# The last product with tokens on the partitions: x and the output gate turned in the gate stage, latent heads first

## What is computed

```python
    n_blocks = S // Q_BLOCK
    mixed = lax.map(attend_block, jnp.arange(n_blocks, dtype=jnp.int32))
    mixed = jnp.transpose(mixed, (1, 0, 2, 3)).reshape(B, S, D_MIX)
    out = (mixed * jax.nn.silu(g)) @ w_out
    return x + gate[:, None, :] * out
```

## Time and profile before

| what | value |
|---|---|
| median of 3 runs | 1884.33 us (1883.67 to 1885.18) |
| the profiled execution, its own time | 1882.65 us |
| its span, first to last instruction | 1880.8 us |
| PE busy | 1803.3 us, 96% of the span |
| DVE busy | 1026.7 us, 55% |
| ACT busy | 624.1 us, 33% |
| mean granted clock of TensorE | 0.976 of full |

### The profile page before, as it was taken

How to read it: one execution, slowest core, us unless ns; L and a number is a source line. 1 busy time by engine, 2 the same in 40 slices (tenths; PEclk the granted TensorE clock), 3 DMA queues, 4 the chain that set the end, 5 groups by cost and what they waited for, 6 DMA issues and landing times.

```text
span 1880.8 us, 22661 instructions
## 1 busy us (share of the span) xinstructions
PE 1803.3 (96%) x9123; PEld 1379.9 (73%) x9123; DVE 1026.7 (55%) x1635; ACT 624.1 (33%) x1038; POOL 70.4 (4%) x84
## 2 busy tenths in 40 slices
PE   7999999999988989999999999999999899898888
PEld 6888888878765567868888888888887554555667
DVE  5665454366366655347344457434445756647663
ACT  4221221321247651342222332222224655225420
POOL 0000000000013220000000000000000000012100
PEclk9999999999889999999999999999999999799989
DMA  6545332262000002213433333233323222101221
GB/s 222 180 157 183 112 91 83 84 204 75 23 1 1 2 22 92 79 56 90 112 90 90 98 109 90 76 115 104 98 78 107 75 78 84 46 23 49 64 90 45
DMA packets 234907, 163.59 MB, mean 87 GB/s; under 512 B 10316, under 2 KB 225588, under 8 KB 234676
## 3 DMA queue, kind: packets, MB, share of 16 engines
q1 hardware_dynamic: 232484, 157.95, 27.5%
q10 hardware_dynamic: 2320, 4.20, 0.6%
HBM read 155.84 MB, written 6.29 MB: 86 GB/s over the span
## 4 chain that ended last, share of the span: by engine, by line
PE 89%; DVE 7%; issue 1%; POOL 1%; ACT 1%; SPq 0%; DMA 0%; ACTq 0%; DVEq 0%
PE bank L896 24%; PE bank L898 23%; PE bank L897 23%; PE bank L1147 3%; PE bank L1135 2%; DVE bank L1857 2%; PE bank L1171 2%; PE bank L1311 2%; PE bank L975 1%; PE bank L1228 1%; PE bank L968 1%; PE bank L1432 1%; PE bank L1443 1%; PE bank L1102 1%; POOL Pm L503 1%
## 5 line engine op out<-in xcount | busy, mean ns | idle before, releaser
L896 PE MATMUL bank<-h_hi,w_hi 128*128 128x512 f32 x1200 | 480.1, 400 | 3.3 <-DVE h_lo L1567 2.1
L898 PE MATMUL bank<-h_hi,w_lo 128*128 128x512 f32 x1200 | 469.0, 391 | 0.0
L897 PE MATMUL bank<-h_lo,w_hi 128*128 128x512 f32 x1200 | 468.8, 391 | 0.0
L559 ACT ACTIVATE w_hi<-w_raw 128x2048 fp32r<-128x2048 f32 (+3 forms) x134 | 236.8, 1767 | 549.3 <-PE bank L898 549.3
L1512 DVE TENSOR_TENSOR w_lo<-w_raw,w_hi 128x2048 fp32r<-128x2048 f32 (+3 forms) x134 | 282.4, 2108 | 62.1 <-ACT w_hi L559 59.3
L896 PEld LDWEIGHTS bank<-h_hi,w_hi 128*128 128x128 f32 x1200 | 226.3, 189 | 75.6 <-issue 25.9
L897 PEld LDWEIGHTS bank<-h_lo,w_hi 128*128 128x128 f32 x1200 | 226.4, 189 | 49.7 <-issue 4.1
L898 PEld LDWEIGHTS bank<-h_hi,w_lo 128*128 128x128 f32 x1200 | 226.0, 188 | 47.7
L896 PE MATMUL bank<-u_hi,w_hi 128*128 128x512 f32 x352 | 138.3, 393 | 0.0
L898 PE MATMUL bank<-u_hi,w_lo 128*128 128x512 f32 x352 | 138.0, 392 | 0.0
L897 PE MATMUL bank<-u_lo,w_hi 128*128 128x512 f32 x352 | 138.0, 392 | 0.0
(11 more groups left out here) (382 smaller groups left out, 2492.3 us busy)
## 6 DMA issues: line engine op xcount, KB each, us to landing
w_raw<-in_w_in SPq DMA_DIRECT2D x28, 1024.0 KB, 5.1
w_raw<-in_ffn_w_gate SPq DMA_DIRECT2D x44, 512.0 KB, 3.7
w_raw<-in_ffn_w_up SPq DMA_DIRECT2D x44, 512.0 KB, 4.8
w_raw<-in_ffn_w_down SPq DMA_DIRECT2D x32, 704.0 KB, 4.5
ada_w<-in_ada_w SPq DMA_DIRECT2D x16, 768.0 KB, 6.2
w_raw<-in_w_in SPq DMA_DIRECT2D x21, 512.0 KB, 3.9
w_raw<-in_w_out SPq DMA_DIRECT2D x8, 1024.0 KB, 5.0
w_raw<-in_w_branch_nsa SPq DMA_DIRECT2D x8, 512.0 KB, 5.0
```

Source lines behind the costliest of these rows:

```text
L559: act.activation(w_hi[s % 2][:, 0:n], w_raw[s % 2][:, 0:n], ACT.Copy).then_inc(s_hi, 1)
L896: pe.matmul(o, l[0], r[0], start=first, stop=False)
L897: pe.matmul(o, l[0], r[1], start=False, stop=False)
L898: return pe.matmul(o, l[1], r[0], start=False, stop=last)
```

## The change

The output product now has z as the stationary operand and w_out as the moving one, so that tokens come out on the partitions and no turning is left behind it. Its slabs are four feature tiles by 512 output columns. Each half of the columns keeps four banks open over two slabs: first with z tiles 4 to 7, then with 0 to 3. Behind it DVE multiplies by a row of gates, adds x and leaves the rest to eight stores of 256 KB.

What this needs is made in the gate stage. After gate tiles 0 to 3 PE turns x, in two groups of four transposes each (`token_rows`, banks 6 and 7), and after gate tile 4 it makes the row of gates on all partitions by eight matmuls of ones with diagonal matrices, which DVE makes from the identity; ACT copies each group out of its bank. The gate tiles are made in the order 4, 5, 6, 7, 0, 1, 2, 3, the latent heads first. The spreading of the four norm rows (`widen`) is divided: two after tile 2, one each after tiles 4 and 5 of that order.

```diff
-        stage("zg", [cols_slab(wz, (c, c + 256)) for c in range(Z_G, Z_G + D, 256)], 8)
-        stage("wout2", [cols_slab(rows(A["w_out_2"][0]), (c, c + 256)) for c in range(0, D, 256)], 8)
-        stage("outT", [], 8)
+        stage("zg", [cols_slab(wz, (Z_G + c, Z_G + c + 256)) for c in (512, 768, 0, 256)], 8)
+        wo2 = rows(A["w_out_2"][0])
+        stage("wout2", [cols_slab(wo2[:, k:k + 4, :], (c, c + 512), kt=4) for c in (0, 512) for k in (4, 0)], 8)
+        stage("end", [], 0)
...
+            for i in range(2 * NT):
+                cols, t = slice(i // NT * 512, i // NT * 512 + 512), i % NT
+                sp.wait_ge(sem("osb_ready"), i + 1)
+                sp.dma_start(out[0, t * P:(t + 1) * P, cols], osb[:, t, cols]).then_inc(sem("out_stored"), 16)
...
+                for b in range(2 * i, min(2 * i + 2, N_ROWS)):
+                    dst = osb[:, b // 2, b % 2 * 512:b % 2 * 512 + 512] if b < 2 * NT else gate_row[:, 512 * (b - 2 * NT):512 * (b - 2 * NT) + 512]
+                    act.wait_ge(sem("row_full"), b + 1)
+                    act.activation(dst, row_bank(b)[:, :], ACT.Copy).then_inc(sem("row_out"), 1)
...
-                    if (s, j) == (1, 0):
-                        pe.wait_ge(sem("sstd"), 5)
-                        for h in range(4):
-                            widen(4, h, 0)
-            pe.wait_ge(sem("z_ready"), 8)
...
+            def token_rows(b):
+                if b >= 2:
+                    pe.wait_ge(sem("row_out"), b - 1)
+                for m in range(4):
+                    o = row_bank(b)[:, m * P:(m + 1) * P]
+                    if b < 2 * NT:
+                        ins = pe.transpose(o, x[:, 4 * (b % 2) + m, b // 2 * P:(b // 2 + 1) * P], ident)
+                    else:
+                        pe.wait_ge(sem("diag_ready"), 4 * (b - 2 * NT) + m + 1)
+                        ins = pe.matmul(o, ones, gate_diag[:, 4 * (b - 2 * NT) + m, :], start=m == 0, stop=m == 3)
+                ins.then_inc(sem("row_full"), 1)
+
+            for i in range(KD):
+                if i % 2 == 0:
+                    wh, wl = use_slab()
+                feature_tile(wh, wl, 0, KD, slice(i % 2 * P, i % 2 * P + P), (h_hi, h_lo))
+                if i == 0:
+                    pe.wait_ge(sem("o_free"), 16)
+                    for h in range(4):
+                        norm_sum(sum_row(0), h, True, True)
+                if i == 2:
+                    pe.wait_ge(sem("sstd"), 5)
+                    widen(4, 0, 0)
+                    widen(4, 1, 0)
+                if i in (4, 5):
+                    widen(4, i - 2, 0)
+                for b in range(2 * i, min(2 * i + 2, N_ROWS)):
+                    token_rows(b)
+            for half in range(2):
+                a0 = acc_at[0]
+                for part in range(2):
+                    wh, wl = use_slab()
+                    for t in range(NT):
+                        if part == 0:
+                            pe.wait_ge(acc_free, a0 + t - 3)
+                        if (half, part, t) == (0, 0, 0):
+                            pe.wait_ge(sem("z_ready"), 4)
+                        tokens = slice(t * P, (t + 1) * P)
+                        for k in range(4):
+                            m = Z_ORDER[4 * part + k]
+                            if (half, part, t) == (0, 1, 0):
+                                pe.wait_ge(sem("z_ready"), 5 + k)
+                            ins = mm3(bank[(a0 + t) % 4][:, :], (z_hi[:, m, tokens], z_lo[:, m, tokens]), (wh[:, k, :], wl[:, k, :]),
+                                      part == 0 and k == 0, part == 1 and k == 3)
+                        if part:
+                            close_acc(ins)
...
+            for i, m in enumerate(Z_ORDER):
+                if 3 <= i < 7:
+                    scaled(diff_out[i - 3], diff_out[i - 3], G_SUB)
+                if i + 1 < KD:
+                    scale_tile(gate_out[(i + 1) % 2][:, :])
...
+                if i < 4:
+                    for k in (2 * i, 2 * i + 1):
+                        tick(dve.tensor_scalar(gate_diag[:, k, :], ident, col[:, G_MOD + 16 + k:G_MOD + 17 + k], None, ALU.mult), "diag_ready")
+                if i % 2:
                     weights_low()
             freed()
-            for t in range(NT):
-                for half in range(2):
-                    copy_tile(osb[:, t, half * 512:(half + 1) * 512])
+            for i in range(2 * NT):
+                cols, t = slice(i // NT * 512, i // NT * 512 + 512), i % NT
+                o = (tmp, tmp2)[i % 2][:, :]
+                if i == 0:
+                    dve.wait_ge(sem("row_out"), N_ROWS)
+                free(dve.tensor_mul(o, take()[:, :], gate_row[:, cols]))
+                freed()
+                done(dve.tensor_add(osb[:, t, cols], osb[:, t, cols], o), "osb_ready")
+                if i in (1, 3):
+                    weights_low()
```

More of the change, by code:

```diff
@@ L276, in build @@
         z_lo = at("z_lo", [P, KD, S], F32R, ARENA + 32 * KB)
-        osb = at("osb", [P, NT, D], F32, ARENA + 60 * KB)
+        osb = at("osb", [P, NT, D], F32, ARENA)
+        gate_row = at("gate_row", [P, D], F32, ARENA + 48 * KB)
+        gate_diag = at("gate_diag", [P, KD, P], F32, ARENA + 52 * KB)
         bias_dram = nc.dram_tensor("bias_scratch", [4, S, S], F32, kind="Internal").ap()
@@ L373, in build @@
         block = ctx.enter_context(nc.Block())
+        Z_ORDER = [4, 5, 6, 7, 0, 1, 2, 3]
+        N_ROWS = 2 + 2 * NT
+        row_bank = lambda b: bank[6 + b % 2]
         rows_of = lambda v: v.rearrange("(k p) -> k p", p=P)
@@ L471, in _ @@
                     load(rbt[:, :], A["rel_bias_2"], "pos_landed")
-            for t in range(NT):
-                sp.wait_ge(acc_free, first_acc["outT"] + 2 * t + 2)
-                sp.dma_start(out[0, t * P:(t + 1) * P, :], osb[:, t, :]).then_inc(sem("out_stored"), 16)
-            sp.wait_ge(sem("out_stored"), 16 * NT)
+            for i in range(2 * NT):
+                cols, t = slice(i // NT * 512, i // NT * 512 + 512), i % NT
+                sp.wait_ge(sem("osb_ready"), i + 1)
+                sp.dma_start(out[0, t * P:(t + 1) * P, cols], osb[:, t, cols]).then_inc(sem("out_stored"), 16)
+            sp.wait_ge(sem("out_stored"), 32 * NT)
         pair_units = lambda hp, ts: [(hp, t, br) for t in ts for br in range(2)]
@@ L1457, in _ @@
             pe.wait_ge(sem("pt_evac"), U0 + len(UNITS2))
[L1458 to L1462, removed]
-                        for h in range(4):
-                            norm_sum(sum_row(0), h, True, True)
-                    if (s, j) == (1, 0):
-                        pe.wait_ge(sem("sstd"), 5)
-                        for h in range(4):
-                            widen(4, h, 0)
@@ L2153, in _ @@
             inverse(5)
[L2154 to L2162, removed]
+            for i, m in enumerate(Z_ORDER):
[3 more added lines that the diff above has]
+                    scale_tile(gate_out[(i + 1) % 2][:, :])
+                dve.wait_ge(sem("zg_ready"), i + 1)
+                if i:
+                    dve.wait_ge(sem("z_ready"), i)
+                done(dve.tensor_mul(tmp[:, :], (diff_out + latent_out)[m], gate_out[i % 2][:, :]))
                 done(dve.tensor_copy(z_hi[:, m, :], tmp[:, :]))
                 done(dve.tensor_sub(z_lo[:, m, :], tmp[:, :], z_hi[:, m, :]), "z_ready")
[L2165 to L2169, removed]
+                if i < 4:
+                    for k in (2 * i, 2 * i + 1):
+                        tick(dve.tensor_scalar(gate_diag[:, k, :], ident, col[:, G_MOD + 16 + k:G_MOD + 17 + k], None, ALU.mult), "diag_ready")
+                if i % 2:
                     weights_low()
             freed()
-            for t in range(NT):
-                for half in range(2):
-                    copy_tile(osb[:, t, half * 512:(half + 1) * 512])
+            for i in range(2 * NT):
[8 more added lines that the diff above has]
+                    weights_low()
 PI32 = 3.1415925
```

## The result

The changed kernel takes 1870.27 us (median of 4 runs, 1868.69 to 1871.62), against 1884.0 us of the kernel before in the same comparison (4 runs, 1882.17 to 1885.18). The ratio is 0.9933, with a 95% interval of 0.9921 to 0.9946: faster by 0.67%, 12.6 us by the ratio (the two medians are 13.7 us apart). The forecast was 10.8 us and 1873.5; 1870.27 lies 0.9 us under the low end of my range, 1871.2, while 0.9933 of the 1884.33 on which the forecast was built is 1871.7, just inside it. The profiled execution has a span of 1868.8 us, 12.0 less than before.

The account below looks back on a forecast made before the run. PE, busy 96%, was taken to bound the kernel. Gains of 4.2 (gate stage), 2.15 (output product) and 4.45 (tail) sum to 10.8 us, giving 1873.5 us from the 1884.33 median; range 1871.2 to 1878.0.

Parts of the forecast that it names:

- The three places: PE's gap at `widen` in the gate stage, the wait and cold start at the output product, and the 9.36 us tail.
- The gate stage: First gate matmul to first output product matmul: 55.05 us forecast against 59.22 before, a gain of 4.2 us.
- The four `widen`: Gate stage term: two took 1.13 us, so four were put at 2.3 us.
- The diagonals' products and the wait at them: After gate tile 4: two groups of four fp32 matmuls, 2.1 us, and PE's new wait for DVE's diagonals, 0.9 us.
- the estimate of 0.22: DVE's time in us for one diagonal by the skill's formula; the forecast kept 0.35 from the nearest row.
- the third slab's margin: Output product: w_lo ready 20.7 us after its start, PE asks at 21.8, so 1 us spare.
- The tail: Behind the last matmul's start: 4.9 us against 9.36, a gain of 4.45; landing with what stands around it 3.0.
- the last step: Own time 1871.85 us raised to 1873.5, as the profiled execution before lay 1.7 us below its median.
- The first, a clock that falls at the new wait: Rival: clock falls behind tile 4, costing 2.15 us and some 1 us for narrow work; 1876.7 us, chance 0.14.
- The second, a late slab: Rival: the output product's first or third slab late, costing 1 to 3 us; 1875.5 us, chance 0.09.
- The third, ACT's copies in the way: Rival: four gate stage blocks each wait about 2 us for banks 6 and 7; 1881.5 us, no change, chance 0.03.
- The fourth, the clock falling at every narrow block: Rival: each of five narrow fp32 blocks costs 2.15 us and its own 1 us again; 1889.2 us, slower, chance 0.04.

Follow-up runs that it names:

- experiments 1: Kernel before, with only the gate tile order (4 to 7, then 0 to 3) and the divided `widen`: 1877.11 us, ratio 0.9969 to the kernel before.
- experiment 2: Changed kernel with diff heads' gate tiles first again and all four `widen` after tile 2: 1876.31 us, ratio 0.9966 to the kernel before.
- experiment 9: Changed kernel with the first two `widen` apart, behind gate tiles 2 and 3: gate stage 55.85 us, 1.26 us longer.
- experiment 5: Changed kernel with the gate row's block behind gate tile 5 and the third and fourth `widen` together there: gate stage 53.41 us, 1.2 us shorter.
- experiment 8: Changed kernel with w_lo of the output product's third slab one token tile later on DVE: output product 44.77 us, 1.5 us longer.
- Experiment 3: Changed kernel with four stores of 512 KB in place of eight of 256 KB: tail 4.94 us in place of 4.31.
- experiment 4: Changed kernel with w_lo of the last gate slab ahead of the last two diagonals on DVE: gate stage 58.42 us, 3.8 us longer.

## Why the prediction was right, and where its sizes were off

**What bounds.** The three places were the right ones: the three terms give 4.63 + 2.16 + 5.05 = 11.84 us of the 12.0 by which the spans differ, and the other 0.16 lie ahead of the gate stage.

**The gate stage**, forecast 55.05, measured 54.59, a gain of 4.6 in place of 4.2. That the order alone takes the standing away is shown by experiments 1 and 2. Inside, five sizes were off and leave only 0.5 us between them, which is partly luck. The 32 transposes took 3.3 us (0.85 and 0.79 for a block of eight), not 3.8. The four `widen` took 1.06 + 1.05 + 1.05 = 3.2, not 2.3: I split the price of a pair by two, and experiment 9 shows that a single one costs the whole 1.05. Tiles 1 to 7 with their edges took 39.1, not 39.3. The diagonals' products and the wait at them took 2.44 together, not 3.0: by experiment 5 the products are 1.8 of that, not 2.1, and the wait cost 0.6, not 0.9. As a row of the timeline it is 0.38. DVE had the first of the two late diagonals 3.35 us after the start of tile 4's last matmul (1799.68 to 1803.03), forecast 3.3; but PE came at 2.97 in place of 2.5, because of the longer `widen`, and the second diagonal was there 0.24 us behind the first (0.48 for two), where I had taken 0.35 from the nearest row. The block ended at 3.81, forecast 3.9. Here the estimate of 0.22 that I worked out from the Trainium skill ("VectorE: DVE Perf Modes", The perf-mode tier table) was nearer than my row.

**The output product**, forecast 43.3, measured 43.29; no wait for any slab, and the third slab's margin 0.9 for 1.0 (experiment 8 shows where it ends). The first slab was in time as well: the last gate matmul at 1820.97 and the first of the product at 1821.20 are one distance apart.

**The tail**, forecast 4.9, measured 4.31. The step that was mis-sized is the landing: from loads of 256 KB, which land in 2.6, I took 3.0 from the last issue to the end of the span, but a store of 256 KB lands in 2.0, and it is 2.4. Experiment 3 gives this difference, 0.63 us, to the size of the store alone. The term makes up half of the 1.2 us by which the sum fell short of the 12.0 between the two spans; 0.4 more are the gate stage, and 0.16 lie ahead of it.

**The time.** The median of 1870.27 lies 3.2 us under the forecast of 1873.5. The sum accounts for 1.2 of them: the profiled execution took 1870.61 us, not 1871.85. The other 2.0 come from the last step. I had added 1.7 because the profiled execution of the kernel before lay that far under its median; that of the change lies 0.3 above its own.

**The rivals.** The first, a clock that falls at the new wait, did not come about at 0.38 us; in experiment 4 it did at 2.58 us, for 1.6 us in place of my 3.2. The second, a late slab, needed the edit of experiment 8. The third, ACT's copies in the way, left no trace: PE has no gap at the blocks. The fourth, the clock falling at every narrow block, is out: the windows are at 1.00 through all five. The swinging clock of "TensorE: Matmul & The Clock Gate" in the Trainium skill (A second HAM failure mode: psum-queue depth-cycling) does not arise in this trace, where the narrow blocks stand without gaps but for that wait.

## What to carry to other kernels

When a narrow, dependent step stands in the program of the busiest engine, look at what is behind it: putting independent work ahead of it cost one reordering and gave half of this gain, and of the same transposes the seven groups that were placed where that engine waits anyway cost nothing; the eighth, behind the last wait, cost 0.4 us. A product whose output lies as the result is stored leaves nothing to be turned behind it, and its last store should be small. Price a wait with the time that the clock may cost behind it, and compare single runs by terms between fixed points of the program, not by spans.

## What the runs showed of the hardware that I had not expected

Two full fp32 matmuls of 32 rows by 512 columns, on different quarters of the partitions and into different banks, take 1.06 us together (the first two in the changed kernel) and 1.05 us alone (experiment 9). The loss of clock can come late: with a gap of 2.58 us the granted clock was still 1.00 in the gap and for about a microsecond of work after it, and only then 0.50, for some 3.4 us (experiment 4). It can also come within the gap (a mean of 0.58 from 1789.00 to 1792.00 in experiment 2, 0.87 before), or not at all: behind 1.88 us of idling the same instructions ran at 0.67 in eight traces and at 1.00 in one. And the size of the last store counts: 2.4 us from its issue to the end at 256 KB, 3.0 at 512 KB (experiment 3).
